# Rotary queries of latent attention: made per head from the latents, or once for all heads, token-major, and kept in DRAM

## The reference, cut to what matters

```python
def rope(x, pos):                  # half-split rotary over the last dim
    ...
    return concat([x1 * cos - x2 * sin, x2 * cos + x1 * sin])

def mla_branch(h, pos, w_in, q_norm, kv_norm, w_uq, w_uk, w_uv, w_out):
    c_q, c_kv, k_pe, z = split(h @ w_in)          # 256, 256, 64, 1024
    c_q, c_kv = rmsnorm(c_q, q_norm), rmsnorm(c_kv, kv_norm)
    q = (c_q @ w_uq).reshape(B, S, 8, 128 + 64)
    q_nope, q_pe = q[..., :128], rope(q[..., 128:], pos)
    k_pe = rope(k_pe, pos)                        # one for all heads
    ...
    # per head: softmax over causal keys of (q_nope . k_nope + q_pe . k_pe) * 192 ** -0.5
    # then the values, a gate silu(z), and w_out
```

## Time and profile before

| | us |
|---|---|
| median of 3 runs (range) | 1426.21 (1425.95 to 1426.92) |
| the profiled execution | 1421.6 |
| its span, first to last instruction | 1419.3 |
| TensorE busy in it | 1335.0 (94%) |
| VectorE, ScalarE, GpSimd busy | 798.1, 554.4, 539.6 |
| second z chunk, about | 127 to 174 |
| layer 0 heads, about | 175 to 475 |

### The profile page before, as it was taken

One profiled execution on the slowest core, in us unless ns is written; L12 is line 12 of the kernel. 1 busy time (PEld: TensorE's weight loads), 2 busy tenths in 40 slices (PEclk: granted clock), 3 DMA queues, 4 the chain that ended last, 5 costly groups with the idle time before them and its releaser, 6 DMA issues.

```text
span 1419.3 us, 19243 instructions
## 1 busy us (share of the span) xinstructions
PE 1335.0 (94%) x7064; PEld 1139.7 (80%) x7064; DVE 798.1 (56%) x1488; ACT 554.4 (39%) x1118; POOL 539.6 (38%) x796
## 2 busy tenths in 40 slices
PE   5999999999999899999997999897989998999997
PEld 4888788989898788888875788776878987888886
DVE  4440155555555515426578889995987776335234
ACT  4321144444444303213334555565156665123122
POOL 3723034544444445334611123323046664734301
PEclk9999999999999999999999999999999999999999
DMA  7122101010110242214400022243122211432112
GB/s 231 45 84 81 45 24 48 33 40 33 33 40 23 83 137 82 71 47 132 134 15 1 31 89 75 90 127 97 45 89 90 75 60 40 136 102 70 58 60 85
DMA packets 70667, 102.20 MB, mean 72 GB/s; under 512 B 6960, under 2 KB 34864, under 8 KB 70576
## 3 DMA queue, kind: packets, MB, share of 16 engines
q1 hardware_dynamic: 70576, 100.99, 22.5%
HBM read 77.37 MB, written 23.59 MB: 71 GB/s over the span
## 4 chain that ended last, share of the span: by engine, by line
PE 74%; DVE 15%; ACT 4%; issue 4%; POOL 2%; DMA 1%; SPq 0%; DVEq 0%; POOLq 0%; ACTq 0%
PE psum L1426 22%; PE psum L1428 22%; PE psum L1427 22%; PE psum L1568 4%; PE psum L1443 2%; ACT psum L1006 2%; DVE gz L1315 2%; DVE xr L1291 2%; DVE p L1116 2%; DVE p L1112 1%; DVE p L1113 1%; PE psum L1454 1%; PE psum L1537 1%; DVE p L1117 1%; POOL p L943 1%
## 5 line engine op out<-in xcount | busy, mean ns | idle before, releaser
L1426 PE MATMUL psum<-ring_hi,act_lo 128*128 128x512 f32 x816 | 323.3, 396 | 10.6 <-issue 5.8
L1428 PE MATMUL psum<-ring_hi,act_hi 128*128 128x512 f32 x816 | 319.5, 392 | 0.0
L1427 PE MATMUL psum<-ring_lo,act_hi 128*128 128x512 f32 x816 | 319.5, 392 | 0.0
L933 POOL CAST ring_hi<-raw 128x512 fp32r<-128x512 f32 x128 | 84.8, 663 | 357.2 <-DMA raw<-in_dsa_w_in 162.4
L1104 DVE TENSOR_TENSOR act_lo<-psum,act_hi 128x512 fp32r<-128x512 f32 (+3 forms) x308 | 176.0, 603 | 70.7 <-ACT act_hi L963 46.6
L1426 PEld LDWEIGHTS psum<-ring_hi,act_lo 128*128 128x128 f32 x816 | 154.4, 189 | 42.2 <-issue 6.0
L963 ACT ACTIVATE act_hi<-psum 128x512 fp32r<-128x512 f32 (+3 forms) x260 | 124.0, 516 | 163.0 <-PE psum L1568 91.8
L942 POOL TENSOR_TENSOR small<-small 128x1 f32<-128x1 f32 x128 | 70.6, 552 | 303.9 <-ACT p L1074 226.8
L936 POOL TENSOR_TENSOR ring_lo<-raw,ring_hi 128x512 fp32r<-128x512 f32 x128 | 179.9, 1406 | 10.3
L1428 PEld LDWEIGHTS psum<-ring_hi,act_hi 128*128 128x128 f32 x816 | 154.3, 189 | 32.9
L1427 PEld LDWEIGHTS psum<-ring_lo,act_hi 128*128 128x128 f32 x816 | 154.6, 189 | 31.1
(11 more groups left out here) (228 smaller groups left out, 2556.0 us busy)
## 6 DMA issues: line engine op xcount, KB each, us to landing
raw<-in_dsa_w_in SPq DMA_DIRECT2D x48, 256.0 KB, 3.1
gz<-z_scratch SPq DMA_DIRECT2D x16, 512.0 KB, 3.5
raw<-in_ple_w_gate SPq DMA_DIRECT2D x32, 256.0 KB, 3.1
raw<-in_mla_w_in SPq DMA_DIRECT2D x24, 256.0 KB, 3.0
xr<-in_x SPq DMA_DIRECT2D x8, 512.0 KB, 5.7
z_scratch<-gz SPq DMA_DIRECT2D x16, 256.0 KB, 2.0
raw<-in_mla_w_out SPq DMA_DIRECT2D x16, 256.0 KB, 3.2
p<-in_x SPq DMA_DIRECT2D x16, 256.0 KB, 3.0
```

Of the source, the lines that this page charges most:

```text
L933: last = nc.gpsimd.tensor_copy(dst, src[:, c0:c0 + cols])
L1426: nc.tensor.matmul(dst, lhs(1), rhs(0), start=start, stop=False)
L1427: nc.tensor.matmul(dst, lhs(0), rhs(1), start=False, stop=False)
L1428: return nc.tensor.matmul(dst, lhs(0), rhs(0), start=False, stop=stop)
```

## The change

- `table_t` goes. In slots 7 and 8 the latents of four tiles each are transposed and split (before: one in each of slots 8 to 15).
- `pe_w` loads, between the chunks, the rotary columns of all eight heads, two pieces of 128 x 512, and splits them into head_w.
- For each token tile t: `pe_proj` (TensorE, six matmuls: tile's latents by all heads' rotary weights, 128 tokens x 512), `pe_turn` (VectorE: rotation by the tables as they are, each head's 64 columns written twice, into p1), `pe_split` (eight transposes; ScalarE writes the scaled high part of all 128 rows to t2, VectorE replaces rows 64 to 127 by the low part there; SP stores t2, 512 KB, to DRAM in pieces of 512 bytes). Projection and rotation of tile t stand in slot 8 + t, its transposes one slot later; the projection of tile 7 in slot 14, its rotation in slot 15, its transposes behind head 0's k.
- Head 0's weights are loaded in slot 14 instead of between the chunks, and v of head 0 stands before its first scores instead of behind them.
- `pe_load` reads one head's rotary queries (128 x 1024, rows of 4 KB) into the high or, for odd heads, the low part of the region. Heads 0 and 1 right behind tile 7's store; head h + 2 at the end of head h, once h's scores are made.
- The scores take two rotary matmuls a chunk, low and high part of the key, instead of three: rows 0 to 63 of the query are high, 64 to 127 low.
- Per head the two "pe" jobs and the exchanged weight columns go.

```diff
@@ z0_extra @@
-        elif k == 5:
-            marks["csq"] = add("table_t", ..., ring="B", jobs=2, freed=["csq"]).after["csq"]
-        elif k >= 8:
-            lo_at["cT"] = split4("xr", 0, ("xn", latent_rows), dest="cT", t=k - 8).after["lo"]
+        elif k in (7, 8):
+            for t in range(4 * (k - 7), 4 * (k - 6)):
+                lo_at["cT"] = lo_at["cT%d" % t] = split4("xr", 0, ("xn", latent_rows), dest="cT", t=t).after["lo"]
+        if 8 <= k < 15:
+            pe_job(k - 8)
+            if k > 8:
+                pe_split(k - 9)
+            pe_turn(k - 8)
+        if k == 14:
+            pe_job(7)
+            head_w.update(enumerate(small_w("head_w", "headW", pieces=3, h=0)))
+        if k == 15:
+            pe_split(6)
+            pe_turn(7)
...
+    def pe_load(h):
+        return add("pe_load", {"pe_ld%d" % (h % 2): 1}, h=h, stored=now["pe_st"],
+                   reader=now["a_full"]).after["pe_ld%d" % (h % 2)]
     z_chunk(0, 2, 0, extra=z0_extra)
-    head_w = dict(enumerate(small_w("head_w", "headW", pieces=3, h=0)))
+    pe_w = small_w("pe_w", "headW", pieces=2)
     z_chunk(0, 3, CW, prefetch=False, extra=z0_extra)
...
-    qk_ready = hproj(0, ["q", "q", "pe", "pe", "k", "k"])
+    qk_ready = hproj(0, ["q", "q", "k", "k"])
+    pe_split(7)
+    pe_at = {h: pe_load(h) for h in range(2)}
+    v_ready = hproj(0, ["v"] * 4)
     pn = {}
...
     first_rows(0, 0)
     first_rows(0, 1)
-    v_ready = hproj(0, ["v"] * 4)
@@ head loop @@
+        if h + 2 < HEADS:
+            pe_at[h + 2] = pe_load(h + 2)
         if more:
             hproj(h + 1, ["q", "q"])
         t_step(0, h, order[6], *pn[6])
-        if more:
-            hproj(h + 1, ["pe", "pe"])
         lo[7] = t_step(0, h, order[7], *pn[7])
@@ SP @@
+                elif k == "pe_split":
+                    sp.wait_ge(sem["lo"], s.after["lo"])
+                    t = n["t"]
+                    sp.dma_start(pe_dram[:, :, t * P:(t + 1) * P],
+                                 t2[:].rearrange("p (h s) -> p h s", s=P)).then_inc(sem["pe_st"], 16)
+                elif k == "pe_load":
+                    sp.wait_ge(sem["pe_st"], n["stored"])
+                    sp.wait_ge(sem["a_full"], n["reader"])
+                    h = n["h"]
+                    sp.dma_start(region(h % 2, PE0, 0, S).bitcast(F32),
+                                 pe_dram[:, h, :]).then_inc(sem["pe_ld%d" % (h % 2)], 16)
@@ ScalarE, VectorE @@
+                elif k == "pe_split":
+                    if s.before["pe_st"]:
+                        act_e.wait_ge(sem["pe_st"], s.before["pe_st"])
...
+                elif k == "pe_turn":
+                    t = n["t"]
+                    dve.wait_ge(sem["b_full"], n["full"])
                     dve.wait_ge(sem["hi"], s.before["hi"])
+                    dup = p1[:].rearrange("p (g r u e) -> p g r u e", r=2, u=2, e=32)
+                    rotate(s, bank(n["bank"]).rearrange("p (g u e) -> p g u e", u=2, e=32), 8, 32,
+                           trig_tile(cos_all, t, 2, 8), trig_tile(sin_all, t, 2, 8),
+                           [dup[:, :, r] for r in range(2)])
@@ TensorE, scores @@
-                            last = product(dst, lambda part: region(part, PE0, qb * P, P),
-                                           lambda part: kpe[part][:, c0:c0 + cn], False, not diag)
+                            if c0 == 0:
+                                pe.wait_ge(sem["pe_ld%d" % (n["h"] % 2)], n["pe_ld"])
+                            for part in (1, 0):
+                                last = nc.tensor.matmul(dst, region(n["h"] % 2, PE0, qb * P, P),
+                                                        kpe[part][:, c0:c0 + cn], start=False,
+                                                        stop=part == 0 and not diag)
```

More of the change, by code:

```diff
@@ L271, in plan @@
     fk = [key_job(0, 1, job).after["fk"] for job in range(2)]
-    rots, marks = [], {}
+    rots = []
     def z0_extra(k):
@@ L278, in z0_extra, with pe_job, pe_turn, pe_split @@
             lo_at["kpeT"] = key_split(0, k - 2, rots[k - 2])
-        elif k == 5:
-            marks["csq"] = add("table_t", {"stage": 2, "b_full": 2, "csq": 2}, ring="B", jobs=2,
-                               freed=["csq"]).after["csq"]
-        elif k >= 8:
-            lo_at["cT"] = split4("xr", 0, ("xn", latent_rows), dest="cT", t=k - 8).after["lo"]
+        elif k in (7, 8):
[12 more added lines that the diff above has]
+            pe_turn(7)
+    def pe_job(t):
+        s = add("pe_proj", {"b_full": 1}, ring="B", jobs=1, freed=["rot_in"], t=t,
+                w_ready=pe_w[-1], c_ready=lo_at["cT%d" % t])
+        pe_full[t] = (s.banks[0], s.after["b_full"])
+        read_by["headW"] = ("b_full", s.after["b_full"])
+    pe_full, pe_rot, head_w = {}, {}, {}
+    def pe_turn(t):
+        pe_rot[t] = add("pe_turn", {"rot_in": 1, "rot": 1}, t=t, bank=pe_full[t][0], full=pe_full[t][1]).after["rot"]
+    def pe_split(t):
+        add("pe_split", {"b_full": 2, "hi": 2, "lo": 2, "pe_st": 1}, ring="B", jobs=2, freed=["lo"], t=t,
+            rot=pe_rot[t])
+    def pe_load(h):
+        return add("pe_load", {"pe_ld%d" % (h % 2): 1}, h=h, stored=now["pe_st"],
+                   reader=now["a_full"]).after["pe_ld%d" % (h % 2)]
     z_chunk(0, 2, 0, extra=z0_extra)
-    head_w = dict(enumerate(small_w("head_w", "headW", pieces=3, h=0)))
+    pe_w = small_w("pe_w", "headW", pieces=2)
     z_chunk(0, 3, CW, prefetch=False, extra=z0_extra)
@@ L319, in hproj @@
         for j, name in enumerate(names):
[L320 to L324, removed]
+            s = add("hproj", {"b_full": 1, "hi": 1, "lo": 1}, ring="B", jobs=1, freed=["lo"], h=h, name=name, j=j if name == "v" else j % 2,
+                    w_ready=head_w[{"q": 0, "k": 1, "v": 2}[name]], c_ready=lo_at["cT"])
         read_by["headW"] = ("b_full", s.after["b_full"])
@@ L752, in small_dest @@
             w = head_w[part]
+            if s.kind == "pe_w":
+                return [(w[:, k * CW:(k + 1) * CW], 0, CW)]
             if s.kind == "ple_w":
@@ L755, in small_dest @@
             if k == 0:
[L756 to L761, removed]
+                return [(w[:, 0:256], 0, 256)]
             if k == 1:
@@ L813, in _ @@
                         sp.dma_start(dst, ple_proj[n["lay"], r * P:(r + 1) * P, j * CW:(j + 1) * CW]).then_inc(ld, 16)
+                    elif k == "pe_w":
+                        r = n["piece"]
+                        sp.dma_start(dst.rearrange("p (h c) -> p h c", h=HEADS),
+                                     w_uq[r * P:(r + 1) * P, :].rearrange("p (h c) -> p h c", h=HEADS)[:, :, NOPE:]
+                                     ).then_inc(ld, 16)
                     elif n["piece"] == 0:
                         h = n["h"]
-                        sp.dma_start(dst[:, 0:384].rearrange("p (r c) -> p r c", r=2),
-                                     w_uq.rearrange("(r p) c -> p r c", p=P)[:, :, h * 192:(h + 1) * 192]).then_inc(ld, 16)
+                        sp.dma_start(dst[:, 0:256].rearrange("p (r c) -> p r c", r=2),
+                                     w_uq.rearrange("(r p) c -> p r c", p=P)[:, :, h * 192:h * 192 + NOPE]).then_inc(ld, 16)
                     elif n["piece"] == 1:
@@ L1051, in _ @@
                     b, j, name = s.banks[0], n["j"], n["name"]
-                    if name == "pe":
-                        act_e.wait_ge(sem["stage"], s.after["stage"])
-                    at = {"q": Q0, "pe": PE0, "k": K0, "v": V0}[name]
+                    at = {"q": Q0, "k": K0, "v": V0}[name]
                     act_e.wait_ge(sem["b_full"], s.after["b_full"])
@@ L1472, in _ @@
                     last.then_inc(sem["b_full"], 1)
-                elif k == "table_t":
+                elif k == "pe_proj":
+                    t = n["t"]
+                    pe.wait_ge(sem["w"], n["w_ready"])
+                    pe.wait_ge(sem["lo"], n["c_ready"])
+                    bank_free(s)
+                    for r in range(2):
+                        last = product(bank(s.banks[0]),
+                                       lambda part: ring[part][:, CT0 + r * S + t * P:CT0 + r * S + (t + 1) * P],
+                                       lambda part: head_w[part][:, r * CW:(r + 1) * CW], r == 0, r == 1)
+                    last.then_inc(sem["b_full"], 1)
+                elif k == "pe_split":
+                    pe.wait_ge(sem["rot"], n["rot"])
                     for j in range(2):
-                        pe.wait_ge(sem["stage"], s.before["stage"] + 1 + j)
                         bank_free(s, j)
                         for i in range(4):
-                            c = j * CW + i * P
+                            c = (4 * j + i) * P
                             last = nc.tensor.transpose(bank(s.banks[j])[:, i * P:(i + 1) * P], p1[:, c:c + P], ident[:])
@@ L1511, in _ @@
                     bank_free(s)
-                    if name in ("q", "pe", "k"):
```

(3 more changed lines are left out.)

28 lines of the change are left out of this document (13 added, 15 removed).

## The result

The changed kernel takes 1402.94 us in the median of four runs (1402.23 to 1403.35), the kernel before 1426.57 (1425.95 to 1429.46): ratio 0.983, 95% interval 0.9815 to 0.9848. On a second chip it was 1400.9 against 1426.4, ratio 0.983 (0.981 to 0.985). So it is 24 us faster where 16.5 were forecast; 1402.9 lies inside the range of 1402.5 to 1420 by 0.4 us.

A forecast was written before the change was run, and what follows sets the result against it. TensorE, busy 94% of the span, was taken as the bound. Work -22.0 us and waits +3.8 gave -18.2; clock +1.7 made -16.5, so 1410 us from the median 1426.2, range 1402.5 to 1420 (8 in 10).

The forecast's parts named there:

- more than forecast: Rival for the whole kernel: head 0's rotary-load wait hidden and fewer stretches at 1.2 GHz, 1404 us; chance 0.10.
- item 4: Head 0's scores wait for the DRAM store and load back: 2.8 us, plus 0.2 for banks, +3.0 us.
- Work of TensorE: Matmuls and transposes, second z chunk and heads: 39.9 us removed, 17.9 us added, net -22.0 us.
- Items 2: Head 0's weights, moved to slot 14: ready before TensorE reaches the projection, no wait, 0.8 us to spare.
- 3: Two old stalls, before head 0's first projection and first scores, go: -1.5 and -1.4 us.
- 5: Head 0's first softmax, no longer covered by v: +2.4 us of waiting, bounds 1.8 and 3.
- 6: Softmax stalls in heads 1, 3, 5 and 7: shorter score tiles cover less, +0.9 us in all.
- 8: Rotary load for head h + 2, waiting on SP for head h's last scores: costs nothing.
- Item 1: Second z chunk: rotary weights, requested after z job 7's store, make TensorE wait 0.4 us, bounds 0 and 1.1.
- Item 7: Head boundary, losing 2.7 us of projection between the transposes of tiles 2 and 3: no wait.
- cover gone at the head boundary: Rival: softmax chain 2 us slower than read, about 1 us lost in eight heads, 1418 us; chance 0.08.
- Clock: One more stretch at 1.2 GHz, added for head 0's wait for its rotary load: +1.7 us, bounds -1.7 and +8.5.

The follow-up runs named there:

- the dead projections: Changed kernel with 14 removed rotary jobs' matmuls put back unread in heads 0 to 6, two ring B banks skipped at layer 1's start: 1422.6 us.
- The two ring experiments: Ring B moved on two banks at layer 1's start: in the changed kernel 1410.29 us, in the kernel before 1415.98 us.

## Why the prediction was right, and where it was not

The sign and layer 0's sum were right, by the mechanism forecast. That the whole time still fell inside the range, by 0.4 us, is luck: 7 to 9 of the 24 us come from behind layer 0's heads, where the sum had nothing. The kernel that the forecast describes, with layer 1's banks as before, is the changed one with ring B moved back; it measured 1410.3 us (on another chip) where 1410 was forecast. The rival "more than forecast" named 1404, but its mechanism, item 4's wait hidden and fewer stretches at 1.2 GHz, did not occur: the wait was there.

- **Work of TensorE, -22.0 us: right.** With the clock taken out, the third pass put back costs 16.1 us (16.4 expected, which holds the 17.3 of the sum), the dead projections 17.4 (17 expected, which holds 19.0 for 14 of the 16 jobs). The z chunk up to head 0's first projection grew by 15.6 us where the steps' sum is 10.9 + 6.1 + 0.4 - 1.5 = 15.9.
- **Items 2, 3, 5, 6 and 8: right.** Head 0's first weights were ready 0.5 us before its first projection. The two old stalls are gone; head 0's softmax is exposed by 2.4 us; the odd heads' stall grew by 0.24 us each. No head after the first waits for its rotary load.
- **Item 1: right size, other cause.** 0.46 us, but not for the weights: the chain goes over ScalarE's and VectorE's split of a tile of latents, whose bank the first rotary projection takes. The weights in 256-byte pieces landed in 3.8 us (median of two), hardly above the 3.6 of the nearest row; the doubling weighed with what the Trainium skill, "DMA: Bandwidth & Descriptors" (Specifications), says of transfers below 512 bytes didn't come.
- **Item 4: the wait for the load right (2.96 against 2.8), its banks wrong.** I counted 0.2 us; it is 2.08, because tile 7's projection, put into slot 14, holds the bank that q's second job takes. That delay reaches both sides of the race: with T at 191.5 us TensorE stood ready at T + 14.5, not 13.0, and the load landed at T + 17.5, not 15.2, so the wait between them kept its size. The loss in front of the scores is 5.0 us, not 3.0. The upper bound of 6.0 was also added wrongly: 8.5 + 4.9 + 4.9 - 13.0 is 5.3.
- **Item 7: wrong.** "Nothing" is 0.7 us in three heads. The slack was read in a head without v weights; in odd heads GpSimd splits these ahead of block 3's normalisation. I had GpSimd's queue in the rows and not in the step. The rival "cover gone at the head boundary" thus came true in part, 2.1 us of its 8, and not by a slower softmax chain but by the order on GpSimd.
- **What was left out: everything behind layer 0.** The forecast took it as unchanged. The two ring experiments put 7 to 9 us on the two-bank shift. This is the step that separates 16.5 us from 24.
- **Clock: +1.7 us, a term that can't be told.** In layer 0 it was 0: both pairs of traces have 6.8 us at 1.2 GHz before and after. The stretch forecast behind item 4's wait is there in the changed kernel's second trace (from 209.8 us on, 3.4 us) and not in its first. Over the whole kernel the first pair shows 10 us more at 1.2 GHz after the change, the second (51 and 38 us) 14 us less, for the same two kernels.

With items 4 and 7 corrected and the clock left out, layer 0's sum is -18.2 + 1.9 + 0.2 + 2.1 = -14.0 us; the traces show -15.5, and the 1.5 us between them stay unexplained. They and the 1.7 us that the clock did not take there made up for most of the 4.2 us that items 4 and 7 lacked; so it is luck, too, that layer 0's 15.5 came so near the 16.5 forecast. With the 7 to 9 us of layer 1 that makes 22.5 to 24.5, the measured 24.

## What to carry to other kernels

A buffer ring handed out by a running count couples stages that share nothing else: when a change adds or removes jobs, work out which buffer each later job gets, and try a bare shift of the count before crediting the change. When work leaves a boundary, look in each engine's queue for what stands ahead of the next result needed, in every variant of the iteration (odd and even heads here). And give a round trip through DRAM its own place in the order: the 7 us for a store and a load of 512 KB cost nothing here once they stood one slot earlier and half of v's projections stood behind the scores.

## What the runs showed of the hardware that was not expected

VectorE's additions from SBUF to SBUF (two inputs, 128 x 256) took up to 0.96 us instead of 0.42 while GpSimd ran a two-input subtraction, and GpSimd's cast went from 0.40 to 0.59. The traces of all thirteen runs hold more of these: 771 such additions with GpSimd's weight work idle took 0.41 to 0.43 us, and 51 that a GpSimd subtraction covered for over 80% of their time took 1.51 us in the median and 1.52 at most. VectorE's multiplications with one input in PSUM (128 x 512) don't suffer: 41 covered in the same way took 0.68 to 0.69 us, as the 334 alone did. The Trainium skill, "GPSIMD Engine Reference" (its table of specifications), says that GpSimd shares its SBUF interfaces with VectorE and contends with instructions of two SBUF inputs; the trace agrees.

The granted clock fell to 1.2 GHz (the lower of its two levels) after the same pair of waits of TensorE (1.3 and 0.9 us) in one execution and not in the next, at the same place in the same kernel: in the first trace of the kernel before it fell behind the stall of head 7 and not of head 5, in the second behind head 5's and not head 7's. A single profile can't price such a stretch as part of a change.
